# Mixture-of-experts block on one core: expert units of 4 MB loaded, waited for and released as two halves

## What is computed

```python
def moe(xn, router_w, router_b, w1, b1, w2, b2):      # 256 x 1024 in; E = 32 experts, D_FF = 1024
    logits = xf @ router_w + router_b
    top_v, top_i = lax.top_k(logits, TOP_K)           # TOP_K = 4
    gates = jax.nn.softmax(top_v, axis=-1)
    ...                                               # rows sorted by expert
    def expert_block(args):
        xb, e = args
        h = xb @ w1[e] + b1[e]                        # w1[e] is 1024 x 2048
        gate, lin = jnp.split(h, 2, axis=-1)
        gate = jnp.minimum(gate, SWIGLU_LIMIT)
        lin = jnp.clip(lin, -SWIGLU_LIMIT, SWIGLU_LIMIT)
        act = gate * jax.nn.sigmoid(SWIGLU_ALPHA * gate) * (lin + 1.0)
        return act @ w2[e] + b2[e]                    # w2[e] is 1024 x 1024
    ...                                               # weighted by the gates and summed per frame
```

## Time and profile before

| | us |
|---|---|
| median of 3 runs | 1285.33 |
| the three runs | 1285.47, 1282.61, 1285.33 |
| the profiled execution's own time | 1286.72 |
| its span, first to last instruction | 1284.5 |
| PE busy | 1214.6 (95%) |
| DVE, ACT busy | 315.9, 199.4 |
| moved by DMA | 445.29 MB |

### The profile page before, as it was taken

One profiled execution on the slowest core, in us unless ns is written; L12 is line 12 of the kernel. 1 busy time (PEld: TensorE's weight loads), 2 busy tenths in 40 slices (PEclk: granted clock), 3 DMA queues, 4 the chain that ended last, 5 costly groups with the idle time before them and its releaser, 6 DMA issues.

```text
span 1284.5 us, 15420 instructions
## 1 busy us (share of the span) xinstructions
PE 1214.6 (95%) x6447; PEld 584.3 (45%) x6448; DVE 315.9 (25%) x783; ACT 199.4 (16%) x374; POOL 14.5 (1%) x52
## 2 busy tenths in 40 slices
PE   6999989999989999999999999999989999999996
PEld 5788877887843333333333333333323333333332
DVE  4554455112132111112121121112111121111212
ACT  2211343012121111111111111111111111111101
POOL 4000000000000000000000000000000000000000
PEclk9999989999999999999999999999999999999999
DMA  8343202573959999999999999999999999999994
GB/s 319 105 153 96 59 3 99 228 295 131 372 207 403 434 428 435 426 438 428 434 432 433 432 432 434 427 438 427 435 431 433 433 431 434 429 436 427 429 427 180
DMA packets 28900, 445.29 MB, mean 347 GB/s; under 512 B 8320, under 2 KB 8704, under 8 KB 10176
## 3 DMA queue, kind: packets, MB, share of 16 engines
q1 hardware_dynamic: 24080, 443.74, 82.0%
q10 hardware_dynamic: 4784, 1.05, 0.4%
HBM read 443.47 MB, written 1.31 MB: 346 GB/s over the span
## 4 chain that ended last, share of the span: by engine, by line
PE 65%; DMA 28%; DVE 3%; ACT 2%; issue 1%; SPq 0%; DVEq 0%; ACTq 0%
PE ps L1337 19%; DMA ring<-in_moe_w 14%; PE ps L1372 13%; DMA arena<-in_moe_w 12%; PE ps L894 9%; PE ps L914 6%; PE ps L1306 3%; PE ps L1288 3%; PE ps L1273 2%; DMA ring<-in_wq_x 1%; PE ps L1294 1%; ACT arena L841 1%; PE ps L1061 1%; DMA ring<-in_w_in 1%; PE ps L1299 1%
## 5 line engine op out<-in xcount | busy, mean ns | idle before, releaser
L1337 PE MATMUL ps<-ring,arena 128*64 128x512 f32 x1248 | 273.8, 593 | 14.6 <-DMA ring<-in_moe_w 13.7
L1337 PE MATMUL ps<-arena 128*64 128x512 f32 x800 | 175.7, 593 | 9.9 <-DMA arena<-in_moe_w 9.9
L1337 PEld LDWEIGHTS ps<-ring,arena 128*64 128x64 f32 x1248 | 88.8, 137 | 195.3 <-issue 172.9
L1372 PE MATMUL ps<-ring,arena 128*64 128x512 f32 x576 | 127.6, 595 | 0.0
L833 ACT ACTIVATE arena<-arena 128x512 f32<-128x512 f32 x31 | 19.5, 630 | 682.9 <-DVE arena L1928 682.9
L1928 DVE TENSOR_SCALAR arena<-ps 128x512 f32<-128x512 f32 x31 | 21.4, 692 | 402.6 <-PE ps L1337 402.6
L1337 PEld LDWEIGHTS ps<-arena 128*64 128x64 f32 x800 | 56.9, 137 | 125.9 <-issue 110.8
L894 PE MATMUL ps<-arena,ring 128*128 128x256 f32 x480 | 107.2, 385 | 2.9 <-DMA ring<-in_wq_x 1.8
L894 PEld LDWEIGHTS ps<-arena,ring 128*128 128x128 f32 x480 | 92.2, 193 | 17.2 <-issue 3.4
L1372 PE MATMUL ps<-arena 128*64 128x512 f32 x416 | 92.3, 595 | 0.9 <-DMA arena<-in_moe_w 0.9
L1941 DVE COPY arena<-ps 128x512 f32<-128x512 f32 x32 | 22.1, 692 | 235.3 <-PE ps L1372 235.3
(11 more groups left out here) (299 smaller groups left out, 900.3 us busy)
## 6 DMA issues: line engine op xcount, KB each, us to landing
ring<-in_moe_w SPq DMA_DIRECT2D x50, 4096.0 KB, 37.5
arena<-in_moe_w SPq DMA_DIRECT2D x33, 4096.0 KB, 37.6
ring<-in_moe_w SPq DMA_DIRECT2D x14, 2048.0 KB, 34.4
arena<-in_moe_w SPq DMA_DIRECT2D x10, 2048.0 KB, 16.8
ring<-in_w_in SPq DMA_DIRECT2D x13, 1024.0 KB, 4.9
ring<-in_wkv_x SPq DMA_DIRECT2D x8, 1024.0 KB, 4.9
ring<-in_w_out SPq DMA_DIRECT2D x4, 1024.0 KB, 4.8
ring<-in_wq_x SPq DMA_DIRECT2D x4, 1024.0 KB, 9.5
```

Source lines behind the costliest of these rows:

```text
L1337: ins = t.matmul(ps[c * BLK:(c + 1) * BLK, 4 + b, :], xeT[:, col:col + BLK], w[:, f0:f0 + 512], start=False, stop=(k == KC - 1), skip_grou ...
L1372: ins = t.matmul(ps[c * BLK:(c + 1) * BLK, 7, :], src[:, col:col + BLK], w[:, f0:f0 + 512], start=(k == 0), stop=(k == KC - 1), skip_group ...
```

## The change

All units are now loaded in two halves of 2 MB with rows of 16 KB, and unit 5 in two halves of two quarters as before. `SPLIT` is gone. Each buffer has two semaphores, `unit{u}_landed` for the first half and `unit{u}_rest_landed` for the second. SP waits for the release of a half of the buffer, issues that half, then does the same for the other. PE waits for the first half before the unit and for the second half after 16 of its 32 matmuls, for every unit. Units 0, 1, 2 and 4, which are loaded before the expert stage, are issued as two DMAs one behind the other.

```diff
-SPLIT = (3, 5, 6, 7, 8, 9, 10)
+        rest_landed = [sem(f"unit{u}_rest_landed") for u in range(SLOTS)]
...
-            def load(n, half=None):
-                sp.dma_start(*unit(n, half)).then_inc(unit_landed[n % SLOTS], 16)
+            def load(n, half):
+                sp.dma_start(*unit(n, half)).then_inc((rest_landed if half else unit_landed)[n % SLOTS], 16)
...
-                    load(early.pop(0))
+                    load(early[0], 0)
+                    load(early.pop(0), 1)
...
-            for n in range(SLOTS + 1, UNITS_ALL - PAIR):
-                if n in SPLIT:
-                    released(n - SLOTS, 0)
-                    load(n, 0)
-                    released(n - SLOTS, 1)
-                    sp.dma_start(*unit(n, 1)).then_inc(sem(f"unit{n}_rest_landed"), 16)
-                else:
-                    released(n - SLOTS)
-                    load(n)
-            for n in load_last():
-                released(n - SLOTS)
+            for n in range(SLOTS + 1, UNITS_ALL):
+                for half in range(2):
+                    released(n - SLOTS, half)
+                    load(n, half)
...
             def arrived(n, landings):
-                pe.wait_ge(unit_landed[n % SLOTS], landings[n % SLOTS] * 16 + (n // SLOTS * 16 + 16))
-                return units[n % SLOTS]
+                count = landings[n % SLOTS] * 16 + (n // SLOTS * 16 + 16)
+                pe.wait_ge(unit_landed[n % SLOTS], count)
+                if n == SLOTS:
+                    pe.wait_ge(sem("unit5_quarter1_landed"), 16)
+
+                def rest():
+                    pe.wait_ge(rest_landed[n % SLOTS], count)
+                    if n == SLOTS:
+                        pe.wait_ge(sem("unit5_quarter3_landed"), 16)
+
+                return units[n % SLOTS], rest
 
-            def first_layer(w, u, before_rest=lambda: None):
+            def first_layer(unit, u):
+                w, rest = unit
                 for k in range(4 * u, 4 * u + 4):
                     if k % 4 == 2:
-                        before_rest()
+                        rest()
...
-            def second_layer(w, src=acT, before_rest=lambda: None):
+            def second_layer(unit, src=acT):
+                w, rest = unit
                 for k in range(KC):
                     if k == 4:
-                        before_rest()
+                        rest()
...
                 for u in range(2):
-                    n = PER * j + u
-                    w = arrived(n, landings)
-                    if n in SPLIT:
-                        pe.wait_ge(sem(f"unit{n}_rest_landed"), 48 if n == SLOTS else 16)
-                    first_layer(w, u)
+                    first_layer(arrived(PER * j + u, landings), u)
```

More of the change, by code:

```diff
@@ L413, in _, with unit @@
             H = UNIT // 2
-            def unit(n, half=None):
+            def unit(n, half):
                 e, t = n // PER, n % PER
@@ L421, in unit, with released @@
                 src, dst = (w1v[e, t] if t < 2 else w2v[e]), units[n % SLOTS]
-                return (dst, src) if half is None else (dst[:, half * H:(half + 1) * H], src[:, half * H:(half + 1) * H])
-            def load(n, half=None):
-                sp.dma_start(*unit(n, half)).then_inc(unit_landed[n % SLOTS], 16)
-            def released(n, half=1):
+                return dst[:, half * H:(half + 1) * H], src[:, half * H:(half + 1) * H]
+            def load(n, half):
+                sp.dma_start(*unit(n, half)).then_inc((rest_landed if half else unit_landed)[n % SLOTS], 16)
+            def released(n, half):
                 e, t = n // PER, n % PER
@@ L446, in _ @@
                     product(sp, "kv7")
-                    load(0)
+                    load(0, 0)
+                    load(0, 1)
                     for i in range(NT):
@@ L473, in _ @@
                 sp.dma_start(b1a[g * E:(g + 1) * E, :], a["moe_b1"][0][:, g * 512:(g + 1) * 512]).then_inc(sem("b1_in"), 16)
-            load(2)
+            load(2, 0)
+            load(2, 1)
             product(sp, "wo0")
@@ L479, in _ @@
             sp.wait_ge(sem("most_squares_ready"), NT)
-            sp.dma_start(*unit(3, 1)).then_inc(sem("unit3_rest_landed"), 16)
+            load(3, 1)
             sp.dma_start(fing[:, :], a["final_g"].unsqueeze(0).to_broadcast([P, D])).then_inc(sem("fing_in"), 16)
-            def load_last():
-                for n in range(UNITS_ALL - PAIR, UNITS_ALL):
-                    yield n
-                    load(n, 0)
[L487 to L493, removed]
-            for n in range(SLOTS + 1, UNITS_ALL - PAIR):
-                if n in SPLIT:
-                    released(n - SLOTS, 0)
-                    load(n, 0)
-                    released(n - SLOTS, 1)
-                    sp.dma_start(*unit(n, 1)).then_inc(sem(f"unit{n}_rest_landed"), 16)
-                else:
-                    released(n - SLOTS)
-                    load(n)
-            for n in load_last():
-                released(n - SLOTS)
+            for half in range(2):
+                dst, src = unit(SLOTS, half)
+                for m in range(2):
+                    sp.wait_ge(eused if m else sem("between_used"), half + 1)
+                    landing = sem(f"unit5_quarter{2 * half + 1}_landed") if m else (unit_landed, rest_landed)[half][0]
+                    sp.dma_start(dst[:, m * SLOT:(m + 1) * SLOT], src[:, m * SLOT:(m + 1) * SLOT]).then_inc(landing, 16)
+            for n in range(SLOTS + 1, UNITS_ALL):
+                for half in range(2):
+                    released(n - SLOTS, half)
+                    load(n, half)
             sp.wait_ge(sem("npass_ready"), 1)
@@ L517, in released_again @@
                             sp.wait_ge(sem("hid_filled" if t == 1 else "yy_filled"), q * E + (e + 1))
-                    for n in range(UNITS_ALL - PAIR):
+                    for n in range(UNITS_ALL):
                         if n >= SLOTS:
                             released_again(n - SLOTS)
-                        load(n)
-                    for n in load_last():
-                        released_again(n - SLOTS)
+                        load(n, 0)
+                        load(n, 1)
             for c in range(2):
@@ L1390, in expert, with last_pair @@
                 bias(it + 1)
[L1391 to L1394, removed]
                 pe.wait_ge(sem("acT_ready"), it + 1)
[L1396 to L1401, removed]
+                second_layer(arrived(PER * j + 2, landings))
+            def last_pair(it, nxt, landings):
                 pe.wait_ge(sem("xeT_ready"), it + 1)
-                first_layer(arrived(0, landings), 0, rest(0))
-                first_layer(arrived(1, landings), 1, rest(1))
+                first_layer(arrived(0, landings), 0)
+                first_layer(arrived(1, landings), 1)
                 move_and_gather(it)
@@ L1412, in last_pair @@
                 pe.wait_ge(sem("xeT_ready"), nxt + 1)
-                first_layer(arrived(2, landings), 0, rest(2))
-                first_layer(arrived(3, landings), 1, rest(3))
+                first_layer(arrived(2, landings), 0)
+                first_layer(arrived(3, landings), 1)
                 pe.wait_ge(sem("acT_ready"), it + 1)
-                second_layer(arrived(4, landings), acT, rest(4))
+                second_layer(arrived(4, landings))
                 pe.wait_ge(sem("gate_ready"), nxt + 1)
@@ L1425, in last_pair @@
                 pe.wait_ge(sem("acT_ready"), nxt + 1)
-                second_layer(arrived(5, landings), acT2, rest(5))
+                second_layer(arrived(5, landings), acT2)
                 pe.wait_ge(sem("sel_ready"), nxt * 2 + 4)
@@ L1444, in _ @@
                         expert(pe.snap(first + j) if j else first, j, landings)
-                last_pair(pe.snap(q_ * E + (E - 2)), pe.snap(q_ * E + (E - 1)), landings_before(q_, E // TURN * PER), q_)
+                last_pair(pe.snap(q_ * E + (E - 2)), pe.snap(q_ * E + (E - 1)), landings_before(q_, E // TURN * PER))
             n_it = pe.snap(np_ * E)
```

## The result

The changed kernel takes 1294.28 us, the median of 7 runs (1289.56 to 1295.34), against 1285.47 us (1282.61 to 1288.12) for the kernel before on the same chip. The ratio is 1.0064, with a 95% interval from 1.0046 to 1.0081: 5.9 to 10.4 us slower. The prediction said 1291.5, from 1288.0 to 1295.2, slower with 84 in 100. Its cause holds; the term for more code, which it took at nothing, and what lies in front of the stream measured more.

A forecast was written before the change was run, and what follows sets the result against it. The continuous stream of expert weights was taken to set the end. Halves added 6.0 us and a later landing ahead of it 0.15, together 6.2 on the 1285.33 median: 1291.5 us, range 1288.0 to 1295.2.

The forecast's parts named there:

- the term for more code: More instructions to load for SP and PE, each load holding one DMA engine: taken as 0, 1 us kept for the range.
- what lies in front of the stream: Before the expert stage, units 1 and 4 queue ahead of query weights PE waits for: that landing comes 0.15 us later.
- The continuous stream: Expert stage from 400 us on: DMA queue never empty, share 1.00 at 432 GB/s; its last landings set the end.
- Two signs: Expected in the changed profile: 2048 KB DMAs landing 37 to 41 us after issue; unit 94's second half landing near 1262.
- The price of a half: Expert weight loads: a unit in halves takes 0.076 us more than whole, bounds 0.05 and 0.11.
- The term of 6.0 us: Units 11 to 89 in the saturated stream: 79 x 0.076 = 6.0 us, bounds 4.0 and 8.7.
- The reading by rows: Unit loads: 8 more, shorter rows on each of 16 DMA engines, 9.5 ns for one extra row.
- Rival B: No change: halves cost extra only in short stretches at the stream's edges; 1285.5 to 1288.5 us, 13 in 100.
- The head start: PE begins a unit's first half about 4.9 us before the second lands; the 3.5 us lead can't be kept: nothing.
- The waits on PE: 90 more waits in the middle of PE's runs, 16 matmuls behind each: nothing; PE has 1.87 us per expert spare.
- the disturbance that the prediction saw at this unit: Second half of unit 92, before the change: 5.37 us by itself while three instruction loads ran; 0.5 us over 4.9.
- the undisturbed price: Extra time per unit in halves without instruction loads, read as 0.080 and 0.071 us; bounds give 1289.4 to 1294.2.

## Why the prediction was right, and where it was off

*What bounds the kernel.* The continuous stream, read from the earlier trace rows, was right. The DMA share stayed at 1.01 with PE's waits moved, joined or doubled, and the time followed the stream's rate in every kernel. Two signs were a little off: the second halves land 41.5 us after their issue, above the 37 to 41 that were named (the medians of all halves are 40.0 and 39.6), and the second half of unit 94 lands at 1264.15 instead of near 1262, for the terms below.

*The price of a half.* The prediction took 0.076 us for a unit; the chain of after gives 9.790-9.713 = 0.077, and the period of 29.37 us is 58.74/2. The term of 6.0 us measured 5.9. The reading by rows, 9.5 ns for each, was an interpretation of two stretches; two kernels now show it: 16 KB in one DMA gives the same stream, and 8 KB the point expected on the line. Rival B, that the price belongs to short stretches at an edge, falls: 79 units paid it in steady flow. The Trainium skill's 3 cycles for a packet ("DMA: Bandwidth & Descriptors", "Why small descriptors are slow"), read as 3.5 ns for a row, is too small against the measured 9.4 to 10.0 ns; the rows of 8 to 32 KB are not what that section is about.

*The head start.* Priced at nothing, and it is nothing: the kernel that gives it up has the same stream and the same span to 0.2 us. *The waits on PE*: nothing in PE's own cycle, likewise.

*In front of the stream.* The prediction had 0.15 us, for two units queued ahead of a DMA that PE waits for. With the low clock in the same places the stage starts 0.5 us later (0.3 to 0.7), but the kernel with one DMA and rows of 16 KB, which pays for the same rows, isn't late. So the mechanism of this small term isn't borne out. What the 0.5 us consists of stays open, and so does whether more than five profiles would still show it.

*More code.* This is the term that was mis-sized. It was taken at 0, with 1 us kept for the range. From unit 88 to the second half of unit 94 the landings are these distances apart (us):

| kernel | loads from 11 to 89 | us |
|---|---|---|
| before, three profiles | whole | 59.1, 59.6, 58.8 |
| waits in the middle | whole | 58.6 |
| rows of 16 KB, one DMA | whole | 58.8 |
| changed, three profiles | halves | 60.1, 59.9, 59.8 |
| halves, PE waits for both | halves | 60.2 |

Unit 89 itself is 0.08 longer in the lower two kinds and in the one with 16 KB. What is left is 0.9 us on average, and four of four with the changed program of SP lie above five of five with the old one, the nearest by 0.1 to 0.2. It is likely the change's, but why it is larger there stays open. It can be placed. In the changed kernel the first half of unit 92 lands at 1239.0 and the second at 1244.6, 5.4 and 5.6 us after the half ahead of each, where an undisturbed half takes 4.9: 1.3 us lost in one unit. In the kernel before, only the second half of unit 92 was late, by 0.5 us. The DMA queues of the changed kernel show three instruction loads between 1229 and 1245 us, as many as before has in its last part:

```profile
q14 instruction: 3, 0.02, 0.4%
```

So the disturbance that the prediction saw at this unit is there in both, and costs more in the changed kernel. Which of the 16 DMA engines such a load holds, and whether it is the slowest one, the profile doesn't tell.

*The place of the clock's low stretches.* The prediction didn't have this at all. It said that the expert stage starts within 0.3 us of 372.0, and it does (371.93), but by luck: the kernel before itself starts it anywhere from 367.57 to 372.00, and the changed kernel at 370.51 when it has one low stretch in front of it instead of two. In the first profile of after the first expert then took 15.65 us for its 64 matmuls instead of 13.95, by the low clock, and the stream began 1.6 us later than in the profile before. These 1.6 of the 8.4 us between the two profiles are the balance of low stretches in different places and of the 0.5 us in front.

The sum by the runs: 5.9 for the stream, 0.9 in the last units, and 0.5 in front if that belongs to the change: 7.3 us, where the prediction had 6.2. The means of all executions on record, at granted clocks that are almost equal, lie 7.9 us apart, the two medians of the first comparison 8.8, and the interval of the measured ratio, 5.9 to 10.4, holds them all. The measured 1294.28 is just above 1294.2, the upper bound of the undisturbed price; it lies in the range by the 1 us that was kept for instruction loads.

## What to carry to other kernels

When a kernel streams its weights without a pause, only the rate and the start of the stream count. Splitting a load so that work can start on the first half then buys nothing, and each extra row is paid on its DMA engine: here 9.4 to 10 ns for each, 0.8% at 16 KB against 32 KB, 2.3% at 8 KB. Split where the queue is about to run dry, as at the units just after the start of the stage (unit 10 showed it here; the last units, split in both kernels, were not tested by themselves), and keep rows as long as the layout allows elsewhere. The price can be read before the edit is made, from landings in a stretch that already has the new form. Before two profiles are subtracted, look where each has its low clock: here that moved the start of the stream by up to 4.5 us between executions of one program.

## What the runs showed that was not expected

A DMA over 64 neighbouring partitions (0 to 63, then 64 to 127, one after the other on one queue) moved 210 GB/s where 128 partitions gave 432, with the same rows of 32 KB and all DMA engines shown busy.

PE's granted clock fell to its lower level for some us in some executions and not in others of the same program. In the profile of after PE had been busy 2.02 of the 4 us before the low stretch at 372 us:

```profile
368.00:372.00 4.00, 2.02 (x12) 0.70 (x10) 2.16 (x12) 2.15 (x3) 0.00 (x0) 1.00 0.00 0
```

Wherever it falls ahead of the stream, at 180 to 204 us, at 362 or at 372, it delays the whole stream; the spans of the changed kernel with the last two and without them lie 3.4 us apart (1292.9 and 1289.5), nearly half of what the change costs, and those of the kernel before with some 10 us of it early and with none 4.6 us (1284.5 and 1279.9).
